# Products that nobody reads, in twelve of the experts' combining steps

## The chip, the cores and the metric

The kernel runs on one core of one Trainium2 chip. The metric is the device time of one execution in microseconds (us), median of several runs. A core has a matrix engine (TensorE, PE in the profile; its weight loads are PEld), a vector engine (DVE), an activation engine (ACT), GpSimd (POOL) and a queue engine (SP) that issues most transfers. PE writes to PSUM, eight banks of 128 partitions by 512 float32 numbers.

## The reference

One decoder block with two token mixers and a mixture of experts, and then two more layers. 256 tokens, width 1024, all float32. What matters here is the mixture of experts between them:

```python
def hier_moe(x, w_group, b_group, w_expert, b_expert, w_gate_up, w_down):
    ...                      # a group of 4, then 2 of its 8 experts for each token, weights from softmaxes
    def expert_block(args):
        xb, e = args
        gate, up = jnp.split(xb @ w_gate_up[e], 2, axis=-1)   # 1024 x 1024
        return (jax.nn.silu(gate) * up) @ w_down[e]           # 512 x 1024
    y_buf = lax.map(expert_block, ...)
    y = jnp.zeros((n_tok, D), x.dtype).at[tok_s].add(y_buf[dest] * w_s[:, None])
```

32 experts have 6 MB of weights each, 201 MB in all, and every one of them is read whichever tokens it gets. Afterwards come a layer norm, a pooling mixer, a feed-forward layer, an attention layer and a second feed-forward layer.

## The kernel before, in words

**Stages.** The program is unrolled, and each engine has its own order, written out by hand, held together by semaphores. From 0 to about 215 us of the span: projections and mixers (weights split into a rounded part and a rest, float32r, three products each: L488 to L490 and L498 to L500) and the router. From about 225 to 660 us: the experts, `pe_experts`, `act_experts` and `dve_experts`, called for experts 0 to 25 and then, behind a branch that the data does not take, for 26 to 31 (`MID = 26`, L2872). Then the second block, where `moving` and `stationary` do most of the work again.

**One expert, e, on PE** (`pe_experts`, L790). Each expert has room for 32 rows. `up(e)`: four units of 1 MB of `w_gate_up`, 64 plain float32 matmul instructions in the records (`blocks`, L835), into bank 4 or 5 (`GB + e % 2`), each waiting for its weights (`loaded`) and the first also for `ht`, e - 1. At odd e from 3 on `combine((e - 3) // 2)` follows: for experts 2q and 2q + 1 the finished rows, in the tile `Y` (rounded part in 32 partitions, rest in 32 more, for two experts), are put to their tokens by a 0/1 tile `SEL`, four float32r products of 512 columns (L890) that accumulate in banks 0 to 3; each pair counts one up on `comb`. Then `down(e - 1)`: two units of `w_down`, 32 instructions (`quarters`, L829), behind waits on the weights, on `ht`, e, and on `y_lo`. Then a piece of the gathering of the next group of four experts (`gather`, L810 and L815) and `turn(e)` (L823), two transposes of the expert's hidden rows.

**The others, for one expert.** ACT: `gate` (L1651) behind the last unit of `up(e)`; `store(e - 1)` (L1659), four roundings of the result into `Y`, behind the last unit of `down(e - 1)` and behind `comb`, since `Y` must have been read. DVE: the product with the gate (L2372, counts `hm`), `store(e - 1)` (L2381, counts `y_lo`), `turn(e)` (L2390, counts `ht`), and at even e `pick` (L2402, L2404), which makes the next `SEL` behind `comb` and counts `pick`.

**Weights.** SP issues all weights in order, each as soon as the unit that had its place is done on PE (`sp_load`, L2793; `sp_two`, L2799, one 2 MB transfer for two units). From `TWICE` on there are ten places of 2 MB, from `LENT` on (the last 32 or so units of the experts) six.

**What the change touches.** `combine` (L884), for q from 1 to 12, that is at e = 5, 7, ... 27.

Of the kernel before, what the change touches and what calls it, by code (L numbers as in the profile page):

```python
# [15 lines left out]
S = 256  # L16
# [752 lines left out]
GB, DB, PB = 4, 6, 7  # L769
# [17 lines left out]
    return (7, 5, 6, 7, 5)[n] if g == 0 else PB  # L787


def pe_experts(pe, K, S, e0, e1):  # L790
    view, bank, con = K.view, K.bank, K.con

# [91 lines left out]
    def combine(q):  # L884

        pe.wait_ge(S.y_lo, 8 * q + 8)
        pe.wait_ge(S.pick, q + 1)
        for i in range(2):
            for c in range(2):
                r = pe.matmul(bank(2 * i + c, 0, [1, 512]), view(K.SEL, 128 * i, [[1, 128]]), view(K.Y, 512 * c, [[1, 512]]),  # L890
                              start=False, stop=False, skip_group_check=True)
            r.then_inc(S.comb, 1)

    def last_combine():
# [37 lines left out]
    for e in range(e0, e1):  # L932
        g = e // 4
        up(e)
        if e == 0:
# [3 lines left out]
            for n in range(4):  # L939
                r = pe.matmul(bank(0, 128 * n, [1, 128]), con("ones"), view(K.DIA, 128 * n, [[1, 128]]), start=True, stop=True)  # L940
# [8 lines left out]
        if e >= 3 and e % 2:  # L949
            combine((e - 3) // 2)  # L950
# [2074 lines left out]
def build(nc, t, out):  # L3025
# [12 lines left out]
    dve_router(dve, K, S, own)  # L3038

    pe_experts(pe, K, S, 0, MID)  # L3040
    act_experts(act, K, S, 0, MID)
    dve_experts(dve, K, S, own, 0, MID)

    overflow(nc, K, S)

    pe_experts(pe, K, S, MID, NE)
    act_experts(act, K, S, MID, NE)
    dve_experts(dve, K, S, own, MID, NE)
# [58 lines left out]
```

## Time and profile before

| | |
|---|---|
| median of 3 runs | 1210.22 us (1205.82 to 1211.85) |
| the profiled execution | 1207.12 us |
| its span | 1205.8 us |
| PE busy | 1067.6 us (89%) |
| DVE, ACT, POOL busy | 580.0, 476.4, 81.8 us |
| mean DMA rate | 274 GB/s over the span |

The profile is of one execution; outside its span lie 1.3 us. Busy shares are means over stages with different limits, and PE's busy time is that of its records, which overlap. The granted clock is 1.0 for TensorE's 2.4 GHz level and 0.5 for its 1.2 GHz level; in a stretch with both the mean stands. A released wait is told in brackets behind a row, as "[idle before <-releaser]".

### The profile page before, as it was taken

Reading aid. Unit: us, or ns where it says so; the run is one execution under the profiler, and the core shown is the slowest. Engines: PE = TensorE matmul, PEld = TensorE weight load, DVE = VectorE, ACT = ScalarE, POOL = GpSimd, SP = SyncE. Lnnn points to the kernel's source line nnn. Section 1 sums busy time; section 2 is a strip of 40 time slices with the busy share of each in tenths; the row PEclk is TensorE's granted clock in tenths of the full one; section 3 lists DMA queues with packets and bytes.
Section 4 is the critical chain, followed back from the end, with each engine's and each line's share of the span. In section 5 each row is a group of like instructions: output and inputs, shape, how many; then the busy total and the mean of one; then the engine's idle time right before and its main releaser. Section 6 shows DMA issues by size and latency. Waiting matters only on the chain.

```text
span 1205.8 us, 21340 instructions
## 1 busy us (share of the span) xinstructions
PE 1067.6 (89%) x9286; PEld 877.5 (73%) x9286; DVE 580.0 (48%) x851; ACT 476.4 (40%) x649; POOL 81.8 (7%) x79
## 2 busy tenths in 40 slices
PE   9999999997666676666678999999999999999998
PEld 8999898754333333333324799999999999999986
DVE  4775775733212121212112776664554548676633
ACT  5644763222111111111123744444357765544433
POOL 1640000000000000000000400000210004000000
PEclk9999999999888878888878999999999999999999
DMA  9843568999999999999999666555534236665530
GB/s 366 309 148 119 179 261 338 397 419 426 427 426 429 425 427 428 427 427 426 418 426 404 224 216 203 175 164 179 182 108 155 89 105 190 207 213 176 176 105 35
DMA packets 104220, 330.28 MB, mean 274 GB/s; under 512 B 4339, under 2 KB 76332, under 8 KB 86334
## 3 DMA queue, kind: packets, MB, share of 16 engines
q1 hardware_dynamic: 102064, 322.77, 69.7%
q10 hardware_dynamic: 1470, 4.02, 0.9%
q0 software_dynamic: 592, 2.10, 0.6%
q8 instruction: 75, 1.23, 0.4%
q14 instruction: 19, 0.16, 0.0%
HBM read 327.82 MB, written 1.06 MB: 273 GB/s over the span
## 4 chain that ended last, share of the span: by engine, by line
PE 64%; DMA 29%; DVE 3%; ACT 2%; issue 1%; SPq 0%; DVEq 0%; ACTq 0%
DMA wide<-in_w_gate_up_dram 22%; PE PS L488 13%; PE PS L490 12%; PE PS L489 12%; DMA wide<-in_w_down_dram 7%; PE PS L1204 5%; PE PS L835 4%; PE PS L498 2%; PE PS L499 2%; PE PS L500 2%; PE PS L829 2%; DVE lo L1962 1%; PE PS L574 1%; PE PS L815 1%; ACT hi L1452 1%
## 5 line engine op out<-in xcount | busy, mean ns | idle before, releaser
L1962 DVE TENSOR_TENSOR lo<-raw,hi 128x2048 fp32r<-128x2048 f32 (+1 forms) x111 | 253.8, 2292 | 143.4 <-ACT hi L1452 120.4
L1452 ACT CAST hi<-raw 128x2048 fp32r<-128x2048 f32 (+1 forms) x109 | 203.7, 1874 | 110.3 <-PE PS L490 75.0
L488 PE MATMUL PS<-AH,hi 128*128 128x256 f32 (+1 forms) x816 | 234.2, 287 | 1.4 <-DVE AL L2453 1.0
L489 PE MATMUL PS<-AL,hi 128*128 128x256 f32 (+1 forms) x816 | 231.4, 284 | 0.0
L490 PE MATMUL PS<-AH,lo 128*128 128x256 f32 (+1 forms) x816 | 231.4, 284 | 0.0
L835 PE MATMUL PS<-wide,XS 128*32 128x256 f32 x1568 | 128.3, 482 | 82.4 <-DMA wide<-in_w_gate_up_dram 79.1
L835 PEld LDWEIGHTS PS<-wide,XS 128*32 128x32 f32 x1568 | 56.1, 131 | 142.8 <-DMA wide<-in_w_gate_up_dram 97.2
L488 PEld LDWEIGHTS PS<-AH,hi 128*128 128x128 f32 x816 | 154.9, 190 | 3.1 <-issue 1.0
L489 PEld LDWEIGHTS PS<-AL,hi 128*128 128x128 f32 x816 | 153.7, 188 | 0.4
L490 PEld LDWEIGHTS PS<-AH,lo 128*128 128x128 f32 x816 | 153.7, 188 | 0.0
L2381 DVE TENSOR_TENSOR Y<-PS,Y 32x256 fp32r<-32x256 f32 x128 | 53.9, 421 | 125.0 <-ACT Y L1659 122.0
L2372 DVE TENSOR_TENSOR T<-T,PS 64x256 f32<-64x256 f32 x32 | 13.5, 423 | 197.3 <-ACT T L1651 197.2
L1659 ACT CAST Y<-PS 32x256 fp32r<-32x256 f32 x128 | 46.5, 364 | 124.8 <-PE PS L829 118.4
L1651 ACT ACTIVATE T<-PS 64x256 f32<-64x256 f32 x32 | 12.1, 378 | 211.5 <-PE PS L835 211.5
L829 PE MATMUL PS<-wide,HT 128*32 128x256 f32 x800 | 62.2, 464 | 37.4 <-DMA wide<-in_w_down_dram 37.4
L829 PEld LDWEIGHTS PS<-wide,HT 128*32 128x32 f32 x800 | 27.4, 127 | 70.5 <-DMA wide<-in_w_down_dram 51.3
L488 PE MATMUL PS<-XH,hi 128*128 128x256 f32 x256 | 73.0, 285 | 0.0
L490 PE MATMUL PS<-XH,lo 128*128 128x256 f32 x256 | 70.9, 277 | 0.0
L489 PE MATMUL PS<-XL,hi 128*128 128x256 f32 x256 | 70.9, 277 | 0.0
L488 PE MATMUL PS<-FH,hi 128*128 128x272 f32 x176 | 50.7, 288 | 0.0
L489 PE MATMUL PS<-FL,hi 128*128 128x272 f32 x176 | 50.7, 288 | 0.0
L490 PE MATMUL PS<-FH,lo 128*128 128x272 f32 x176 | 50.5, 287 | 0.0
(430 smaller groups left out, 1856.4 us busy)
## 6 DMA issues: line engine op xcount, KB each, us to landing
wide<-in_w_gate_up_dram SPq DMA_DIRECT2D x49, 2048.0 KB, 45.7
wide<-in_w_down_dram SPq DMA_DIRECT2D x25, 2048.0 KB, 45.5
raw<-in_ffn_w_gate_dram SPq DMA_DIRECT2D x22, 1024.0 KB, 5.5
raw<-in_ffn_w_up_dram SPq DMA_DIRECT2D x22, 1024.0 KB, 5.7
raw<-in_w_in_dram SPq DMA_DIRECT2D x21, 1024.0 KB, 8.8
raw<-in_ffn_w_down_dram SPq DMA_DIRECT2D x19, 1024.0 KB, 5.0
spare<-in_w_gate_up_dram SPq DMA_DIRECT2D x14, 1024.0 KB, 12.7
raw<-in_sb_w_qkv_dram SPq DMA_DIRECT2D x12, 1024.0 KB, 5.2
```

Of the source, the lines that this page charges most:

```text
L488: pe.matmul(o, w(h, c), xh(k), start=start and c == c0, stop=False)
L489: pe.matmul(o, w(h, c), xl(k), start=False, stop=False)
L490: r = pe.matmul(o, w(l, c), xh(k), start=False, stop=stop and c == c0 + len(ks) - 1)
L498: pe.matmul(o, xh(k), K.view(h, n * c, [[1, n]]), start=start and c == c0, stop=False)
L499: pe.matmul(o, xl(k), K.view(h, n * c, [[1, n]]), start=False, stop=False)
L829: r = pe.matmul(bank(b, 0, [1, 256], p0=32 * c, rows=32), x, view(w[0], w[1] + 256 * c, [[1, 256]]), start=first, stop=last)
L835: r = pe.matmul(bank(b, 0, [1, 256], p0=32 * c, rows=32), x, view(w[0], w[1] + 512 * (c // 2) + 128 * (c % 2), [[256, 2], [1, 128]]), star ...
L1204: r = pe.matmul(bank(last_bank(i, p), 0, [1, 512]), x, view(y, D * c + 512 * p, [[1, 512]]), start=False, stop=k == 21 and a == 2, skip_gr ...
L1452: act.copy(K.view(K.hi[i % HN], 0, [[1, n]]), K.view(K.rbuf[i], 0, [[1, n]])).then_inc(S.hi, 1)
L1659: act.copy(view(K.Y, 256 * c, [[1, 256]], 64 * (e % 2), KEEP), bank(down_bank(e), 0, [1, 256], p0=32 * c, rows=KEEP)).then_inc(S.y_hi, 1)
L1962: r = e.tensor_tensor(K.view(K.lo[i % HN], 0, [[1, n]]), K.view(K.rbuf[i], 0, [[1, n]]), K.view(K.hi[i % HN], 0, [[1, n]]).bitcast(F32), A ...
L2381: dve.tensor_tensor(l, bank(down_bank(e), 0, [1, 256], p0=32 * c, rows=KEEP), h.bitcast(F32), ALU.subtract).then_inc(S.y_lo, 1)
```

## The change

In twelve combining steps PE waits for `ht`, 2q + 3, and runs further products into bank 4 (`GB`), which the next `up` overwrites. The `comb` count of the second pair moves behind them.

```diff
+FORMS = (("round", 0, 128), ("round", 0, 64), ("round", 0, 512), ("round", 48, 256), ("round", 16, 256), ("round", 32, 256),
+         ("whole", 0, 256), ("whole", 0, 128), ("round", 0, 384), ("round", 0, 272), ("round", 0, 192), ("round", 0, 16),
+         ("wait", 0, 0), ("round", 0, 240), ("round", 8, 256))
+PER_STEP = 5
+
+
+def pe_keep_warm(pe, K, S, b, q):
+
+    view, bank = K.view, K.bank
+    upper, lower = (view(K.Y, at, [[1, 128]]) for at in (656, 784))
+    rows = lambda a: view(K.Y, 256 * a, [[1, 256]])
+
+    def triples(n):
+
+        for _ in range(n):
+            for w, a in ((upper, 0), (upper, 1), (lower, 0)):
+                r = pe.matmul(bank(b, 0, [1, 256]), w, rows(a), start=True, stop=True)
+        return r
+
+    triples(2)
+    for n in range(PER_STEP):
+        kind, at, width = FORMS[(PER_STEP * (q - 1) + 4 * ((q - 1) // 3) + n) % len(FORMS)]
+        if kind == "round":
+            pe.matmul(bank(b, 0, [1, width]), upper, view(K.Y, at, [[1, width]]), start=True, stop=True)
+        elif kind == "whole":
+            pe.matmul(bank(b, 0, [1, width]), K.con("ident"), view(K.cm, 0, [[1, width]]), start=True, stop=True)
+        else:
+            pe.wait_ge(S.pick, q + 1)
+        r = triples(2)
+    return r
+
+
@@ in combine(q)
             for c in range(2):
                 r = pe.matmul(bank(2 * i + c, 0, [1, 512]), view(K.SEL, 128 * i, [[1, 128]]), view(K.Y, 512 * c, [[1, 512]]),
                               start=False, stop=False, skip_group_check=True)
+            if i and 1 <= q <= 12:
+
+                pe.wait_ge(S.ht, 2 * q + 3)
+                r = pe_keep_warm(pe, K, S, GB, q)
             r.then_inc(S.comb, 1)
```

## Rows read from the trace of the kernel before

**Rows 1.** The page: rate of the DMA and granted clock in 40 slices of the span
```profile
PEclk9999999999888878888878999999999999999999
DMA  9843568999999999999999666555534236665530
GB/s 366 309 148 119 179 261 338 397 419 426 427 426 429 425 427 428 427 427 426 418 426 404 224 216 203 175 164 179 182 108 155 89 105 190 207 213 176 176 105 35
```

**Rows 2.** Busy time by stretch: us, PE, PEld, DVE, ACT, POOL, PEclk, DMA share, GB/s
```profile
280.00:600.00 320.00, 210.89 (x2344) 110.70 (x2332) 71.86 (x198) 48.35 (x127) 0.00 (x0) 0.83 1.01 426
600.00:650.00 50.00, 35.73 (x354) 15.85 (x354) 9.54 (x26) 12.79 (x25) 0.00 (x0) 0.80 1.01 426
```

**Rows 3.** The chain that ended last: start us, us, what
```profile
314.84 47.18 DMA wide<-in_w_gate_up_dram
...
561.39 29.41 DMA wide<-in_w_gate_up_dram
590.80 0.04 issue
590.85 2.49 PE PS L835 x32
...
622.59 27.39 DMA wide<-in_w_gate_up_dram
649.98 0.04 issue
650.03 3.60 PE PS L835 x32
```

**Rows 4.** PE's groups from 271 to 597 us: busy, mean ns, idle before
```profile
L835 PE MATMUL PS<-wide,XS 128*32 128x256 f32 x1312 | 105.2, 475 | 74.6 <-DMA wide<-in_w_gate_up_dram 71.3 <-issue 3.3
L829 PE MATMUL PS<-wide,HT 128*32 128x256 f32 x656 | 52.1, 471 | 31.8 <-DMA wide<-in_w_down_dram 31.8
```

**Rows 5.** SP's 74 transfers of 2 MB: time from issue to landing
```profile
DMA to landing us min/median/max: 24.6/45.6/48.9
```

**Rows 6.** PE in order of time, at the combining step q = 1
```profile
271.32 1.21 PE L890 MATMUL PS<-Y,SEL 128*128 128x512 f32 x4
272.46 1.93 PE L829 MATMUL PS<-half,HT 128*32 128x256 f32 x32
...
282.19 1.07 PE L829 MATMUL PS<-spare,HT 128*32 128x256 f32 x16 [1.09 <-DMA spare<-in_w_down_dram]
...
287.15 1.07 PE L835 MATMUL PS<-spare,XS 128*32 128x256 f32 x16 [0.64 <-DMA spare<-in_w_gate_up_dram]
292.07 3.43 PE L835 MATMUL PS<-wide,XS 128*32 128x256 f32 x32 [3.84 <-DMA wide<-in_w_gate_up_dram]
```

**Rows 7.** The same at the last step, q = 12
```profile
593.24 2.08 PE L890 MATMUL PS<-Y,SEL 128*128 128x512 f32 x4
596.13 1.93 PE L829 MATMUL PS<-wide,HT 128*32 128x256 f32 x32 [0.81 <-DMA wide<-in_w_down_dram]
597.99 0.71 PE L810 MATMUL PS<-SW,cm 128*128 128x128 f32 x4
598.63 0.34 PE L823 MATMUL PS<-cm,T 64*128 64x64 f32 x2
601.01 2.39 PE L835 MATMUL PS<-wide,XS 128*32 128x256 f32 x32 [2.04 <-DMA wide<-in_w_gate_up_dram]
605.91 3.52 PE L835 MATMUL PS<-wide,XS 128*32 128x256 f32 x32 [2.50 <-DMA wide<-in_w_gate_up_dram]
```

**Rows 8.** The chain in two dense stretches, for the cost of a product
```profile
57.78 1.78 PE PS L574 x16
65.02 1.78 PE PS L574 x16
...
272.54 1.86 PE PS L829 x32
274.40 1.98 PE PS L815 x16
...
656.88 1.92 PE PS L927 x8
```

**Rows 9.** Instruction queue from 280 to 600 us: packets, MB, share of 16 engines
```profile
q8 instruction: 20, 0.33, 0.4%
```

**Rows 10.** PE in order of time, first expert behind the branch
```profile
570.12 1.27 PE L835 MATMUL PS<-wide,XS 128*32 128x256 f32 x17
574.67 4.48 PE L835 MATMUL PS<-wide,XS 128*32 128x256 f32 x47 [3.29 <-issue]
```

**Rows 11.** By stretch again (columns of rows 2): PE dense, and two pairs of experts
```profile
260.00:265.00 5.00, 5.00 (x89) 2.98 (x81) 1.97 (x5) 1.73 (x5) 0.00 (x0) 1.00 1.00 415
359.20:388.60 29.40, 17.42 (x205) 8.15 (x206) 7.86 (x23) 3.98 (x12) 0.00 (x0) 0.83 1.00 426
388.50:417.90 29.40, 20.89 (x233) 11.46 (x233) 5.54 (x14) 4.84 (x12) 0.00 (x0) 0.83 1.01 427
```

## The prediction

> **What bounds the kernel now.** I read the slices of the page first, then a table by stretch, then the chain of waits, and only then single rows at the place of the change. The reader is to see in the slices that the transfers are at 426 GB/s or so for some twelve slices of 30 us, and that this is also where the granted clock is below full [rows 1]. The table by stretch says it in one row: from 280 to 600 us all 16 DMA engines are busy (share 1.01), 426 GB/s, while PE has work in 211 of 320 us, at a mean clock of 0.83 [rows 2]. The chain of waits goes there through transfers alone: 47, 29 and 27 us each, joined by one half of an `up` whose end frees a place [rows 3]. PE stands still for weights before L835 and L829, 71.3 and 31.8 us, 103 us in the stretch that holds the twelve steps [rows 4]. So the experts take as long as their 201 MB take, and the question is only whether PE's new work can hold up a transfer, or the end.
>
> **How far PE may fall behind.** A transfer of 2 MB lands 24.6 us after its issue at the least, 45.6 in the median [rows 5]; at 427 GB/s it needs 2.097 MB / 427 GB/s = 4.9 us itself. So when PE frees a place, five to nine transfers are still ahead of it. PE can free a place 24.6 - 4.9 = 19.7 us later than now at the worst place, and the DMA engines still do not run dry. In the last part, with six places, the chain's 27.4 us [rows 3] leave 22.5 us.
>
> **What the change adds.** Each step has 2 + 5 x 2 = 12 triples, 36 float32r products of 256 columns with a weight load each. In the dense projections 48 such products stand between two groups of L574: 65.02 - (57.78 + 1.78) = 5.46 us, 0.114 us each, loads hidden [rows 8]. 36 x 0.114 = 4.10 us. The odd products: the index runs through all 15 forms once in three steps, four times in all. Twelve rounded ones have 128 + 64 + 512 + 3 x 256 + 384 + 272 + 192 + 16 + 240 + 256 = 2832 columns; at 0.114 / 256 = 0.445 ns a column that is 1.26 us. The two float32 ones: L927 has eight records for four products of 256 columns in 1.92 us, 0.48 us each; L815 has eight products of 128 columns in 1.98 us, 0.25 us each [rows 8]. Together 1.26 + 0.73 = 1.99 us in three steps, 0.66 us a step. A step costs 4.76 us, twelve cost 57 us. That is at the full clock. The L835 group in the chain takes 3.60 us at its worst and a warm group of the same size about 1.9, as L829's 1.86 [rows 3, 8], so a step wholly at the lower level costs up to double, 9.5 us.
>
> **Where this lies.** 57 us against 103 us of standing still for weights [rows 4]; even twelve steps at the lower clock, 114 us, exceed that by 11 us only, less than the 19.7 us that PE may fall behind. Step by step: at q = 1 the products start at about 272.5 and push `down(4)` by 4.8 us; the idle times behind it are 1.09, 0.64 and 3.84 us, 5.6 in all, so at 292.07 PE waits for the same landing as before [rows 6]. At q = 12 they start at 594.4 (L890 overlaps the next start by some 0.1 us, or 595.3 by its record) and end by 600.1; `down(26)` then starts 4 us late, and with 1.93 + 0.64 + 0.34 us for it, the gathering and the turn PE reaches `up(28)` at 603 instead of 601.0; its first half ends at 605.4 at the latest, before the next weights land at 605.91 [rows 7]. There the lag is gone, 44 us before the last wait that is on the chain, at 650.0 [rows 3]. On the path: nothing.
>
> **The new waits and the moved count.** `ht`, e, is waited for by `down(e - 1)` right behind anyway; it was counted before `up(e)`, which takes two landings. The second wait, on `pick`, has been passed at the head of `combine`. Both cost nothing. `comb` comes 4.8 us later. Behind it wait ACT's and DVE's `store(e - 1)`, which need `down(e - 1)`, and this stands behind the products on PE; DVE's `pick` at e + 1 stands behind its `turn(e + 1)`, later still. Nobody waits longer than for PE itself. ACT's `gate(e)` waits for the unit ahead of the combining step and is not moved. Bank 4 is free: what `ht` counts is its last reader.
>
> **Costs that the trace does not show.** First the instructions: 432 + 48 products and 8 float32 ones of two records each, 496 matmuls and as many loads, 992 instructions. From 280 to 600 us 0.33 MB of instructions came for some 5,000 records, 66 bytes each [rows 2, 9]; 992 make 65 KB, and as the DMA engines are full these are 65 KB / 427 GB/s = 0.15 us, on the path. Second, a stall for instructions: the row behind the branch has one of 3.3 us in the middle of an `up` [rows 10]. Lower bound 0; upper bound four more of these, 13 us in all, but inside the slack above; I take 0. Third, whether products slow the transfers: 415 GB/s with PE dense, but with 1 MB transfers; between pairs of experts with 17.4 and 20.9 us of PE it is 426 and 427 [rows 11]. Lower bound 0, upper bound the 136 MB of this stretch at 415 in place of 426: 320 x (426 / 415 - 1) = 8.5 us. I take 0, by the nearer rows. Fourth, the clock: the products fill gaps, so less of PE's work meets the lower level. On the path that can only be the 3.60 us group behind 650.0, up to 1.7 us, and no product is added behind 600; I take 0.
>
> The row of the stall may be weighed against the Trainium skill, Runtime: NRT & Kernel Launch, "Instruction fetch mechanics": the sequencer fetches the next page of instructions by itself while it runs the present one, mostly hidden, and a taken branch breaks this. By the rule the straight-line products cost no stall at all; by the row alone one could fear 3.3 us for each new page. The sum is the same either way, since PE has the slack.
>
> **Sum.** The profiled execution: 1207.12 + 0.15 = 1207.3 us. It stands 3.1 us under the median of the runs, so the forecast is 1207.3 + 3.1, about 1210 us. The three runs shown lie 6 us apart, 0.5%, which is also about what a measurement of this kernel can tell from no change.
>
> **The rivals.** (a) The warmer clock shortens the experts. For it: clock 0.83 means that 0.34 of 320 us, 109 us, is at the lower level [rows 2]; PE is busy two thirds of that, and half of this, 36 us, would be won if PE set the pace, 1174 us. Against it: DMA share 1.01 throughout, so the work would end earlier only to wait longer. Chance 0.03. Here the Trainium skill, TensorE: Matmul & The Clock Gate, "Why this matters for your kernels", speaks for the change: keep TensorE busy and leave no idle gaps between bursts of matmuls for the most throughput. The rule may well hold for the clock, and by it the time would be this rival's. (b) The products slow the transfers, because both read or write the same memory, or by instructions fetched through the same engines: the bound above, 8.5 us, 1219 us. For it: the 415 of the dense stretch. Against it: 426 and 427 whatever PE does. It decides at a mean rate below 419 GB/s from 280 to 600 (320 x 7 / 419 = 5.3 us). Chance 0.09. (c) PE becomes the bound: the products run at the lower clock or with stalls, more than 103 us in all and over 19.7 us behind at one place. With nothing hidden it is 57 us, 1267 us. Chance 0.03. That makes 0.15 for the three. (d) The change does not do what it is named for: the clock stays at 0.83, because gaps remain at the even experts. Time as forecast; within the forecast I give it 0.3. The forecast has 0.85.
>
> **How the numbers follow.** Within 0.5% is 1204 to 1216. Of the forecast's 0.85, spread of runs alone takes 0.03 to each side; with (a) faster has 0.06; with (b) and (c), and the part of (b) that stays under 6 us taken out, slower has 0.13; same 0.81. The range holds the forecast with the spread of runs below it, 1204, and the smaller half of (b) above it, 1217.
>
> **What the profile of the changed kernel would show.** PE busy from 280 to 600 rises from 211 to 250 to 265 us (57 less what the warmer clock takes off the rest); its wait for weights before L835 and L829 falls from 103 to 45 to 65 us; the new products take 4.7 to 6 us a step; mean clock 0.86 to 0.95; rate 425 to 427 GB/s; the last wait for `w_gate_up` in the chain still ends at 649 to 651 us. Wrong would be a rate under 422, an idle time of the DMA engines behind a step, or a chain that goes through PE between 300 and 640.

## The result, and the profile after

| | before | after |
|---|---|---|
| median of 20 runs | 1205.8 us (1204.8 to 1211.85) | 1210.55 us (1206.65 to 1214.17) |
| the profiled execution | 1207.12 us | 1211.29 us |
| its span | 1205.8 us | 1210.0 us |
| PE busy | 1067.6 us (89%) | 1112.8 us (92%) |

The ratio of the times is 1.0023, with an interval of 1.0013 to 1.0034: the change makes the kernel slower by about 2.8 us (1.6 to 4.1). The two medians lie further apart, 4.75 us, because the times of either kernel scatter over 7 us; the ratio is what the rest goes by. The forecast of 1210 us fits the time after within a microsecond, but that is luck: it was built on a median of three runs, 1210.22 us, which twenty runs put at 1205.8 us. What it said of the *change*, 0.15 us, was too little.

The page after, with rate and granted clock in 40 slices [rows 1]:

```profile
PEclk9999999999888889788888999999999999999999
GB/s 368 278 163 117 191 241 357 376 418 425 428 426 428 426 427 426 428 425 428 417 426 400 232 208 194 191 140 174 187 94 159 119 105 156 209 224 192 181 103 35
```

The stretches of [rows 2], after:

```profile
280.00:600.00 320.00, 251.96 (x2834) 164.76 (x2827) 72.49 (x199) 48.69 (x127) 0.00 (x0) 0.88 1.01 426
600.00:650.00 50.00, 38.12 (x409) 18.61 (x407) 10.86 (x29) 14.19 (x30) 0.00 (x0) 0.86 1.00 426
```

PE works 41 us more in the same 320 us, at a mean clock of 0.88 in place of 0.83, and the transfers run at the same 426 GB/s. Its groups from 273 to 599 us and what ended the idle time before them [rows 4] (L867 and L861 are the former L835 and L829, L922 the former L890, L806 the triples, L813 and L815 the odd products):

```profile
L867 PE MATMUL PS<-wide,XS 128*32 128x256 f32 x1312 | 92.2, 431 | 37.8 <-DMA wide<-in_w_gate_up_dram 36.8 <-DVE HT L2426 0.9
L806 PE MATMUL PS<-Y 128*128 128x256 f32 x403 | 57.1, 286 | 0.0
L861 PE MATMUL PS<-wide,HT 128*32 128x256 f32 x640 | 49.2, 460 | 30.3 <-DMA wide<-in_w_down_dram 30.3
```

Standing still for weights has fallen from 103.1 to 36.8 + 30.3 = 67.1 us. The first step in order of time, and a piece behind it [rows 6]:

```profile
273.26 1.21 PE L922 MATMUL PS<-Y,SEL 128*128 128x512 f32 x4
274.31 0.85 PE L806 MATMUL PS<-Y 128*128 128x256 f32 x6
...
278.48 0.86 PE L806 MATMUL PS<-Y 128*128 128x256 f32 x6
279.27 1.93 PE L861 MATMUL PS<-half,HT 128*32 128x256 f32 x32
...
294.63 1.72 PE L867 MATMUL PS<-wide,XS 128*32 128x256 f32 x28 [1.75 <-DMA wide<-in_w_gate_up_dram]
...
597.78 1.08 PE L806 MATMUL PS<-Y 128*128 128x256 f32 x6
...
603.03 1.93 PE L861 MATMUL PS<-wide,HT 128*32 128x256 f32 x32
...
608.35 1.93 PE L867 MATMUL PS<-wide,XS 128*32 128x256 f32 x32 [0.61 <-DMA wide<-in_w_gate_up_dram]
...
653.24 3.40 PE L867 MATMUL PS<-wide,XS 128*32 128x256 f32 x32 [1.90 <-DMA wide<-in_w_gate_up_dram]
```

A step takes 279.27 - 274.31 = 4.96 us at q = 1 and 603.03 - 597.78 = 5.25 us at q = 12, and behind each the next weights find PE waiting again (294.63, 608.35). The chain of waits [rows 3] is no longer transfers and single groups alone: from 324 to 340, 384 to 399, 443 to 459, 503 to 520 and 593 to 605 us it goes through PE, with the products of a step in it each time. Pieces of it, and its end in this stage:

```profile
451.60 1.51 PE PS L806 x12
...
459.15 43.88 DMA wide<-in_w_gate_up_dram
503.07 3.40 PE PS L867 x32
...
516.91 3.63 PE PS L867 x64
520.56 42.13 DMA wide<-in_w_gate_up_dram
...
564.73 28.76 DMA wide<-in_w_gate_up_dram
...
605.02 22.84 DMA wide<-in_w_down_dram
...
629.90 28.22 DMA wide<-in_w_down_dram
658.17 1.93 PE PS L861 x32
```

Whether PE hid the products all the same, the experiments have to tell. The last wait for `w_gate_up` ended at 653.24 us, not at 650.03. Of these 3.2 us, 1.94 are older than the change: the L890/L922 product at the first combining step stood at 271.32 and now stands at 273.26. That leaves 1.3 us in a stage in which PE waits for transfers and transfers run at full rate. One thing that has changed there shows in the instruction queue of PE, here from 228 to 650 us (packets, MB, share of 16 engines), before and after:

```profile
q8 instruction: 29, 0.48, 0.5%
```

```profile
q8 instruction: 33, 0.54, 0.5%
```

### The profile page after: what moved, and what is told of

It is laid out like the page before. It is cut to its first block, busy times and chain, and to the rows that moved or that the text cites. A ratio compares the mean times of both kernels' runs of the same rounds, so it can differ in the third digit from the quotient of the medians.

```text
span 1210.0 us, 22332 instructions
## 1 busy us (share of the span) xinstructions
PE 1112.8 (92%) x9782; PEld 936.7 (77%) x9782; DVE 580.1 (48%) x851; ACT 476.9 (39%) x649; POOL 84.0 (7%) x79
## 4 chain that ended last, share of the span: by engine, by line
PE 68%; DMA 25%; DVE 3%; ACT 2%; issue 1%; SPq 0%; DVEq 0%; ACTq 0%
DMA wide<-in_w_gate_up_dram 20%; PE PS L488 13%; PE PS L489 12%; PE PS L490 12%; PE PS L1240 5%; PE PS L867 4%; DMA wide<-in_w_down_dram 4%; PE PS L806 2%; PE PS L861 2%; PE PS L498 2%; PE PS L499 2%; PE PS L500 2%; PE PS L847 1%; DVE lo L1998 1%; PE PS L574 1%
## 5 line engine op out<-in xcount | busy, mean ns | idle before, releaser
L867 PE MATMUL PS<-wide,XS 128*32 128x256 f32 x1568 | 113.1, 440 | 42.6 <-DMA wide<-in_w_gate_up_dram 41.7
L867 PEld LDWEIGHTS PS<-wide,XS 128*32 128x32 f32 x1568 | 52.0, 123 | 93.1 <-DMA wide<-in_w_gate_up_dram 55.1
L861 PE MATMUL PS<-wide,HT 128*32 128x256 f32 x800 | 60.6, 454 | 37.4 <-DMA wide<-in_w_down_dram 37.3
L2408 DVE TENSOR_TENSOR T<-T,PS 64x256 f32<-64x256 f32 x32 | 13.5, 423 | 140.7 <-ACT T L1687 140.6
L861 PEld LDWEIGHTS PS<-wide,HT 128*32 128x32 f32 x800 | 26.8, 125 | 63.7 <-DMA wide<-in_w_down_dram 44.2
L806 PE MATMUL PS<-Y 128*128 128x256 f32 x432 | 61.0, 286 | 0.0
L806 PEld LDWEIGHTS PS<-Y 128*128 128x128 f32 x432 | 57.8, 191 | 1.8
```

The lines of the kernel that those rows point to most:

```text
L806: r = pe.matmul(bank(b, 0, [1, 256]), w, rows(a), start=True, stop=True)
L861: r = pe.matmul(bank(b, 0, [1, 256], p0=32 * c, rows=32), x, view(w[0], w[1] + 256 * c, [[1, 256]]), start=first, stop=last)
L867: r = pe.matmul(bank(b, 0, [1, 256], p0=32 * c, rows=32), x, view(w[0], w[1] + 512 * (c // 2) + 128 * (c % 2), [[256, 2], [1, 128]]), star ...
```

## The experiments

One profile is not enough for 1 us, so each number below is read alike from every profile. "Anchor" is an instruction of DVE in the router, a fixed one, 2.97 us behind PE's first gathering product (the expectations count from that product, so their landing times are 3.0 us larger than mine). "Landing" is when the last share of the last 2 MB of `w_gate_up` is there (the records show each transfer landing in sixteen shares), "spread" the time from its first share to its last. "Stage" runs from the anchor to a DVE instruction behind the last expert. FFN1 is a fixed piece of the first feed-forward layer, which the change does not touch. Pages are the packets of q8 from the anchor up to that landing, 16 KB each. Worked out from the traces, us:

```
kernel        span     stage   landing  spread  pages  FFN1
before        1205.8   436.45   421.2    6.7     29    108.61
b1_same       1206.0   436.88   421.6    7.0     29    108.59
b2_same       1211.4   438.86   421.7    6.9     29    111.53
b3_same       1206.3   438.49   421.3    6.8     29    108.59
b4_same       1207.9   436.73   421.5    6.9     29    108.59
b5_same       1204.7   437.08   421.9    7.3     29    108.59
after         1210.0   437.73   422.5    7.6     33    111.54
a1_same       1205.9   438.74   422.5    8.1     33    108.58
a2_same       1212.6   441.68   423.3    8.8     33    111.54
a3_same       1212.7   439.64   422.7    8.1     33    111.54
a4_same       1206.8   439.57   422.7    7.8     33    108.58
a5_same       1209.3   438.97   422.7    7.9     33    108.59
n1_narrow     1208.5   438.12   422.9    8.2     33    111.15
s8_waits      1208.2   437.92   422.7    7.9     33    111.53
w1_wide       1204.4   436.83   421.6    6.9     31    108.59
s4_waits      1204.4   436.80   421.6    6.7     31    108.59
c8_act_waits  1204.5   437.04   421.8    7.4     29    108.58
```

**The same two kernels again: b1_same to b5_same, a1_same to a5_same.** No edit; one profile each, a1_same also timed. Expected of the first two pairs:

> The kernel before, unchanged, for a second profile of it. In the two first profiles PE's float32r products follow each other at a steady distance that differs by stage and by kernel: 123.3 ns (before) against 126.7 ns (after) in the first feed-forward layer's hidden products, 117.8 against 113.3 ns in the second one's. Theory P (place): the distance belongs to the program, by where its instructions or tiles lie: this run shows 123.3 and 117.8 ns again. Theory E (execution): it is drawn anew in each execution: this run shows other values. Theory X (the experts): neither matters, and all of the added 2.8 us lie in the experts' stage.

> The changed kernel, unchanged, for a second profile and for more times. Theory P: 126.7 and 113.3 ns again. Theory E: other values, drawn from the same few. Theory X: the way from the first combining step to the last wait of the experts is 1 to 3 us longer than in the second profile of the kernel before. All three expect a ratio of about 1.0023.

> The kernel before once more, for a third profile. Theory I: 29 pages, 424.2 to 424.8 us. Theory E: anywhere from 424 to 426.

> The changed kernel once more, for a third profile of the experts' stage. Theory I: 33 pages again, the last gate and up landing at 425.4 to 425.7 us behind the first gathering. Theory E (the stage is drawn anew in each execution): anywhere from 424 to 426.

Measured: a1_same 1208.31 us against 1207.67 us, ratio 1.0016 (1.0002 to 1.0030), so slower again, if barely. FFN1 took 111.53 us in b2_same and 108.58 us in a1_same, so theory P falls: the distance of its products does not belong to the program. The six landings of each kernel do not overlap: 421.2 to 421.9 before, 422.5 to 423.3 after, means 421.53 and 422.73, 1.2 us apart. The stages are 437.42 and 439.39 us in the mean, 2.0 us apart; they overlap. The stage varies more because some of PE's last groups run at the lower clock in some executions of either kernel. The tail of a2_same in order of time, the costliest:

```profile
647.94 3.64 PE L867 MATMUL PS<-wide,XS 128*32 128x256 f32 x32 [4.40 <-DMA wide<-in_w_gate_up_dram]
651.51 3.62 PE L945 MATMUL PS<-PMM,MT 16*128 16x32 f32 x16
655.05 3.64 PE L867 MATMUL PS<-wide,XS 128*32 128x256 f32 x32
658.63 1.99 PE L922 MATMUL PS<-Y,SEL 128*128 128x512 f32 x4
```

Here 32 instructions take 3.64 us, right behind a wait of 4.40 us; the same group takes 1.93 us where PE is warm.

**n1_narrow: the same instructions, each with 16 columns.**

```diff
-    rows = lambda a: view(K.Y, 256 * a, [[1, 256]])
+    rows = lambda a: view(K.Y, 256 * a, [[1, 16]])
...
-                r = pe.matmul(bank(b, 0, [1, 256]), w, rows(a), start=True, stop=True)
+                r = pe.matmul(bank(b, 0, [1, 16]), w, rows(a), start=True, stop=True)
```

(and the odd products at most 16 columns wide)

> All added products cut to 16 columns: the number of instructions, their order and the waits stay, PE's added time falls from 5.0 us a step to 1.2 to 2.5 us. Theory P: the distances are those of the changed kernel (126.7 and 113.3 ns), and the ratio stays at about 1.002. Theory X: the added work is what delays the experts, the ratio falls to 1.000 to 1.001. Theory E: ratio anywhere from 1.000 to 1.003, distances unlike either profile.

**w1_wide: half as many products in the triples, twice as wide.**

```diff
-    rows = lambda a: view(K.Y, 256 * a, [[1, 256]])
+    rows = lambda a: view(K.Y, 256 * a, [[1, 512]])
...
-    triples(2)
+    triples(1)
```

(and the same in the loop)

> Six products of 256 columns become three of 512: PE's added time stays, the added instructions fall from 992 to 560. Theory X: ratio as for the changed kernel, 1.002. Theory P: the stream lies elsewhere, so the distances differ from both profiles and the ratio with them, 0.998 to 1.004. Theory E: distances drawn anew, ratio about that of the changed kernel.

Measured: n1_narrow 1209.19 us, ratio 1.0014 (1.0000 to 1.0028); w1_wide 1207.01 us, ratio 1.0003 (0.9990 to 1.0016). The cut of n1_narrow failed as a cut of PE's work. Its third step in order of time:

```profile
326.34 0.73 PE L806 MATMUL PS<-Y 128*128 128x16 f32 x6
...
330.87 1.43 PE L806 MATMUL PS<-Y 128*128 128x16 f32 x6
332.23 3.22 PE L862 MATMUL PS<-wide,HT 128*32 128x256 f32 x28
```

From 326.34 to 332.23 it takes 5.89 us, longer than a step of the change at q = 1 (4.96 us): with a load of its own each, one product of 16 columns follows the other after 0.11 us and, where the granted clock is 0.50, after 0.21 us and more. All twelve steps together take 72.3 us, against 60.8 us in the kernel after. But the number of instructions is what was kept, and with it the 33 pages and the landing at 422.9. w1_wide is the better test, for its PE does the same work in columns and its twelve steps take the same time, 60.4 us, at an even higher clock; the stretch of [rows 2] for the two:

```profile
280.00:600.00 320.00, 267.81 (x2826) 180.47 (x2822) 72.55 (x199) 48.66 (x127) 0.00 (x0) 0.81 1.01 426
```

```profile
280.00:600.00 320.00, 242.57 (x2639) 150.26 (x2641) 72.53 (x199) 48.21 (x126) 0.00 (x0) 0.91 1.01 426
```

The second is w1_wide: clock 0.91, PE 242.57 us, 31 pages, and the landing is back at 421.6. Its chain of waits goes through the products of a step just as the changed kernel's does:

```profile
451.14 1.51 PE PS L806 x6
...
458.69 42.72 DMA wide<-in_w_gate_up_dram
```

PE's work, its delay of 5 us a step and its traffic to the memories therefore cost nothing at the landing; the number of instructions is what is left.

**s8_waits: no products at all, only instructions.** The kernel before, and in `combine`:

```diff
+        if 1 <= q <= 12:
+            for _ in range(171):
+                pe.wait_ge(S.pick, q + 1)
```

> The kernel before with no products at all, but 171 waits that have long been passed behind each of the twelve combining steps: 2052 more PE instructions, eight more pages of 16 KB on the instruction queue. Theory I (instruction pages): a page takes one DMA engine for 1.07 us, the pages go round through eight engines, every 2 MB transfer has landed only when the slowest of its 16 shares has; so eight more pages cost one full round, 1.1 to 1.5 us: the last gate and up landing moves from 424.2 or 424.7 us behind the first gathering to 425.3 to 426.5, and the ratio is 1.001 to 1.0015. Theory X (the products' work delays the experts): no products, so no change, 424.2 to 424.7 and 1.000. Theory B (bytes only, shared by all engines): 131 KB / 427 GB/s = 0.3 us.

The 2052 waits make only 1032 instructions more (two share one), four pages and not the eight that I had counted: 4 x 16 KB for 2052 waits are 32 bytes each, half of the 66 bytes of an instruction. Measured: 1208.16 us, ratio 1.0009 (0.9996 to 1.0022), by itself no finding. The stage tells more. PE does none of the products:

```profile
280.00:600.00 320.00, 202.90 (x2412) 115.92 (x2412) 72.54 (x199) 48.55 (x127) 0.00 (x0) 0.82 1.01 426
```

and yet it has 33 pages and the landing at 422.7 with a spread of 7.9, as in the kernel after. The waits are passed at once and take up to 7.2 us a step (42 ns each), 81.7 us in all, which the weights hide as they hide the products.

**c8_act_waits: the instructions on another engine.** In `act_experts`, behind the gathering:

```diff
+        if 5 <= e <= 28:
+            for _ in range(86):
+                act.wait_ge(S.silu, e)
```

> The same number of passed waits in ACT's stream, 86 for each of the experts 5 to 28, 2064 in all. Theory I, if ACT's pages go through the same engines: as s8_waits, 1.1 to 1.5 us; if they go through others or in smaller pieces, nothing. Theory X: nothing. Theory B: 0.3 us.

ACT's queue (q14) brings 14 pages in place of 6, of 8 KB each:

```profile
q8 instruction: 29, 0.48, 0.5%
q14 instruction: 14, 0.11, 0.1%
```

Measured: 1208.37 us, ratio 1.0008 (0.9997 to 1.0018). The landing is at 421.8, at the upper edge of the kernel before, with a spread of 7.4, just above all of its six. Eight small pages of another queue cost some 0.3 us by that; one profile can't tell this from nothing.

**s4_waits and s12_waits: fewer and more.** s4_waits is s8_waits with `range(86)`. s12_waits has this behind `up(e)` and the combining step, ahead of `down(e - 1)`:

```diff
+        if 3 <= e <= 28:
+            for _ in range(126):
+                pe.wait_ge(S.ht, e - 1)
```

> Half of s8_waits: 86 passed waits behind each of twelve combining steps, 516 more instructions, two pages, as w1_wide without its products. Theory I: the next step of the slowest engine falls behind the last weights, so they land at 421.2 to 421.9 us as before, ratio 0.999 to 1.001. Theory L: half of what s8_waits costs, 0.6 us. Theory E: 421 to 424.

> The kernel before with 126 passed waits at each of the experts 3 to 28, 3276 in all; as two waits share an instruction (2052 of them made 1032 more), 1638 more instructions, six to seven pages, no products. Theory I: 35 or 36 pages in the stage; the slowest DMA engine takes one more page than before, like with 33, but the step comes earlier, so the last gate and up weights land 1.0 to 1.5 us later than before (422.6 to 423.3 us behind the anchor where before has 421.2 to 421.7), ratio about 1.001. Theory L (linear in pages): 1.5 times what 33 pages cost, 1.8 us. Theory E: 421 to 424 whatever is added.

s4_waits: 1206.89 us, ratio 1.0010 (1.0000 to 1.0019), 31 pages, landing 421.6. A price by the byte or by the page would have put the landing halfway; it is a step. The step shows in the landings alone: in the timed runs s4_waits, s8_waits and c8_act_waits (1.0010, 1.0009, 1.0008) can't be told apart, nor from no change. s12_waits missed its aim: 1216.82 us, ratio 1.0108 (1.0083 to 1.0133), because there PE itself became the bound. Its waits by releaser from 270 to 660 us (in all, times, longest), and its second stretch of [rows 2]:

```profile
PE PS L829 <- issue: 133.3, 25, 6.3
```

```profile
600.00:650.00 50.00, 35.30 (x358) 17.72 (x358) 8.69 (x22) 8.55 (x21) 0.00 (x0) 0.72 0.91 366
```

133 us of passed waits against 103 us in which PE stood still [rows 4]: this is what rival (c) of the prediction looks like, with a DMA share of 0.91 and 366 GB/s. Its theories were all missed (the last `w_gate_up` lands at 428.9 us, with a spread of 0.5 us), and on the pages this kernel says nothing.

**Which page does it.** The kernels with 31 pages equal those with 29, and those with 33 are 1.2 us later. So I set the arrival of single pages beside the gaps between landings of 2 MB (4.9 us apart as a rule), us behind the anchor:

```
kernel     9th, 17th, 25th, 33rd page       landings after a gap over 5.5 us
before      92.3  226.6  350.1  480.6        98.6  232.3  351.1  357.2
w1_wide     87.7  211.6  334.9  447.8        89.9  213.8  337.5  352.9
s4_waits    87.6  211.5  336.6  449.4        89.7  213.6  342.3  348.0
s8_waits    86.7  197.7  315.5  416.4        89.3  203.4  317.6  357.4  422.7
after       82.2  197.0  312.9  416.8        84.4  203.2  317.3  352.8  422.5
```

Of the 22 long gaps 18 come 1 to 7 us behind a 9th, 17th, 25th or 33rd page; the other four lie at 348 to 357 us, just behind the branch, where pages come closer together in every kernel. The 33rd comes behind the last weights (421) in the first three kernels and ahead of them in the last two. The last `w_gate_up` transfer of the kernel after shows it at close range, its last six shares counted from the first one, 5.7 us before and then itself:

```
the transfer that lands at 416.8   6.2 6.5 6.6 6.6 6.7 6.7
the one that lands at 422.5        ... 6.6 6.7 6.7 7.6
```

Fifteen shares are as before and one is 0.9 us late. In s8_waits the same pair ends 6.9 and 7.9.

That pages go round eight engines can be counted in the shares. Here are the nine latest of the sixteen at the last `w_gate_up` landing, us behind the first share; the other seven lie within 1.9 us of it:

```
kernel    pages   shares
before      29    3.2   4.6 5.0 5.2   6.1 6.1 6.2 6.6 6.7
s4_waits    31    3.1   4.8   5.9 6.1 6.4 6.4 6.5 6.6 6.7
w1_wide     31    3.3   4.9   6.2 6.3 6.3 6.4 6.4 6.5 6.9
s8_waits    33    3.3   5.7 6.2 6.3 6.3 6.4 6.4 6.9   7.9
after       33    2.9   5.9 6.2 6.5 6.6 6.6 6.7 6.7   7.6
```

Eight shares are late and eight are not. Three rounds of eight are 24 pages; 29 are 5 more, and five shares are over 5.5 us late; 31 are 7 more, and it is seven; with 32 it is all eight, and the 33rd page puts one share beyond the rest. This holds in each of the 16 profiles with 29, 31 or 33 pages and no pages added on ACT's queue; in c8_act_waits nine shares are over 4 us late in place of eight, and six over 5.5 us.

**a3 to a5, b3 to b5.** Three more profiles of each kernel, for the rest of the stage and for FFN1:

> The changed kernel, a fourth profile. Theory I: last gate and up weights at 422.4 to 423.4 us. For the distance of products in the first feed-forward layer: 126.7 ns if the change favours it (3 of the 4 so far), 123.3 as likely as not if it does not.

> The kernel before, a fourth profile. Theory I: last gate and up weights at 421.2 to 421.8 us. Distance of products in the first feed-forward layer: 123.3 ns if the state goes with the kernel (2 of 3 so far), else either.

> The changed kernel, a fifth profile. Theory I: last gate and up weights at 422.4 to 423.4 us. Theory G (the state of the first feed-forward layer goes with the kernel): its middle part takes 111.5 us. Theory N (it does not): 108.6 or 111.5 us, as likely.

> The kernel before, a fifth profile. Theory I: 421.2 to 421.8 us. Theory G: the middle part of the first feed-forward layer takes 108.6 us. Theory N: either.

> The changed kernel, a sixth profile. Theory I: last weights at 422.4 to 423.4 us; theory G: 111.5 us; theory N: either.

> The kernel before, a sixth profile. Theory I: last weights at 421.2 to 421.8 us; theory G: 108.6 us; theory N: either.

They are in the first table: theory I held within 0.1 us, theory G fell (a4_same and a5_same have 108.6 us). The mean spans of the six and six are 1207.0 and 1209.5 us, 2.5 us apart, near the 2.8 of the timed runs. By parts: stage +2.0; FFN1 +1.0 (111.5 instead of 108.6 us in 1 of 6 before and 3 of 6 after); the second feed-forward layer 0.0; the first 80 DVE instructions, ahead of the change, -0.5. Of the stage's 2.0 us, 1.2 is the landing and 0.8 lies behind it: from the landing of `down(30)` to the end of the stage it is 10.97 us in the mean before and 11.71 after (10.3 at the least in both, 13.5 in a2_same). Whether the change has any part in FFN1 stays open: all kernels with 33 pages that I profiled have the longer one in 5 of 8 cases, the others in 1 of 9. No cause was found for it, and so few cases may be chance. The 0.8 us stay as open: all of them come from executions in which further groups of PE ran at the lower clock, five of the eight with 33 pages and two of the nine others. The changed kernel's own first profile, n1_narrow and s8_waits land as late and have the shortest tail, 10.3 us.

## Why the prediction was right or wrong

**What bounds the experts, and the room PE has.** Right. The rate stayed at 426 GB/s and the DMA share at 1.01. One of my signs for "wrong" did appear: the chain goes through PE between 300 and 640 us, from 503.07 to 520.54 for instance, with a step in it. The sign was badly chosen; before the change, too, the chain goes once through several groups of PE, from 461.09 to 468.79 us. Such a stretch only says which group of PE freed the place of a transfer that then stood 42 us in a full queue. The queue never ran dry: the shortest way from issue to landing of a 2 MB transfer fell from 24.6 to 22.8 us, against the 4.9 us that it needs itself, and w1_wide has the same chain, 22.2 us, and the landing of the kernel before. (Of the 24.6 us 19.7 lie before the transfer's own time, so four transfers at the least are ahead of it, not the five that I wrote; nothing hangs on it.) The last wait for `w_gate_up` in the chain missed its 649 to 651 us, since it ended at 653.24; 1.94 us of this lie ahead of the change. w1_wide and s8_waits show the sum "on the path: nothing" for PE's part: work of 5 to 7 us a step is hidden whole. The end of the room lies between the 82 us of s8_waits, which were hidden, and the 133 us of s12_waits, which were not; the 103 us of standing still fit in between. Rival (c) falls with this.

**The price of a step.** Predicted 4.76 us, measured 4.72 to 5.62; PE's 57 us are 60.8. Its busy time, 252 us, lies in the 250 to 265 forecast, the clock, 0.88, in 0.86 to 0.95. The wait for weights, 67 us, ended 2 us above the 45 to 65. Rivals (a) and (d) fall: the clock did rise, 0.83 to 0.88, in w1_wide to 0.91, and no time came of it. Here the advice in the Trainium skill, TensorE: Matmul & The Clock Gate, "Why this matters for your kernels", holds for the clock and not for the time, as said.

**The step that failed.** It is the first of the "costs that the trace does not show": "992 make 65 KB, and as the DMA engines are full these are 65 KB / 427 GB/s = 0.15 us, on the path". The mechanism is the one named there, and in rival (b) ("by instructions fetched through the same engines"); the term was mis-sized, and rival (b) looked for it in the wrong number, the rate. It spreads the bytes over sixteen engines. But a page is one packet of 16 KB, and the rows were there to size it: 0.4% of 16 x 320 us is 20.5 us for 20 packets [rows 9], 1.0 us of one engine each. A transfer of 2 MB counts as landed when the slowest of its sixteen shares is in. Early in the stage, 2.4 us behind the anchor, they come in within 0.7 us; at its end the last is 6.7 to 8.8 us behind the first. Only what the slowest engine has to do beside the weights moves the end; the rest lands in engines with time to spare. A price per page would have been 4 x 1.0 = 4 us; the average over engines 0.15 us. The measured one, 1.2 us, is one page on the slowest engine. That the pages go round eight engines is read from the counts of late shares and from the gaps behind the 9th, 17th, 25th and 33rd page; the records do not name the engine of a page. This step explains the 1.2 us of the landing, and not all of the 2.8 us that were timed: the rest is open.

On instruction fetch I had weighed the Trainium skill, Runtime: NRT & Kernel Launch, "Instruction fetch mechanics" (the next page is fetched while the present one runs, mostly hidden). Hidden from PE it was: no new stall for instructions shows in the rows of PE from 273 to 599 us. It is not hidden from the transfers, which the rule does not speak of.

**The end.** I took 0 for the clock at the last groups. The tail is 0.8 us longer in the mean. What makes it longer in an execution is the clock: groups of 3.6 us for 1.93 behind a wait (a2_same above), in b2_same and b3_same too. That the change brings this about is not shown, since n1_narrow and s8_waits, as late, have none of it.

**The base.** The three runs shown were 1205.82, 1211.85 and 1210.22; their median lay 4.4 us too high. The profile's own 1207.12 us was the better base: 1207.12 plus 2.8 is 1209.9 us, and with the 0.15 us of the prediction it would have been 1207.3.

The difference of the six and six spans, then, 2.5 us: 1.2 us shown (landing), 0.8 us in the tail and 1.0 us in FFN1, of which it is open whether the change has a part in them, less 0.5 us from ahead of the change. The timed difference is 2.8 us (1.6 to 4.1), and 1.9 us by the ratio of a1_same, so what is shown is roughly half of it.

## What to carry to other kernels

In a stage in which all DMA engines are full, instructions are traffic too (shown here for PE's; ACT's smaller pages could not be told from nothing). Count them in pages, by the packets of the instruction queues, and price a page on one engine, and on the slowest one; not as bytes over all sixteen. Where weights bound a stage, look at how far apart the shares of its last transfer land: this spread, and not the mean rate alone, set the end here. And fill PE's gaps for the clock only where PE is the bound: here the clock rose by 0.05 to 0.08 for nothing.

## What the runs showed of the hardware

- A float32r product of 16 columns with a weight load of its own is not shorter than one of 256: 0.11 us at a granted clock of 1.00, 0.21 us and more at 0.50, so n1_narrow had more PE time (267.8 us) than the change (252.0 us), at a lower clock (0.81).
- A wait that is passed at once costs PE 42 ns (7.2 us for 171 in s8_waits; 5.5 us for 126 in s12_waits), and two of them take one instruction.
- The products of FFN1, 272 columns each, come 123.3 ns apart in some executions and 126.7 ns in others, of the same kernel, all at a granted clock of 0.9 or more; over FFN1 that is 108.6 or 111.5 us. The second feed-forward layer has such a pair too, independent of the first: from its norm to its last hidden product 104.8 or 108.2 us. With the tail of the experts (10.3 to 13.5 us) and the time ahead of them (DVE's 81st instruction starts at 115.4 to 117.7 us) this makes up most of the scatter between executions of one kernel.
- The shares of a 2 MB transfer drift apart from 0.7 to some 7 us over 420 us of full rate: eight of the sixteen by a step for each of PE's pages of instructions, 1.0 us of an engine's time each, the other eight by 3.7 us at most.
